# Three weight tiles in place of two, row by row, behind four of the six norms

## The reference

```python
hx = _modulate(_rms(x, norm_mix_g[i]), sx1, cx1)          # rms norm, then (1 + scale) * h + shift
x = x + gx1 * mixer(hx, ...)                              # layer 0: conv/Fourier; layer 1: attention
x = x + gx2 * _mlp(_modulate(_rms(x, norm_mlp_g[i]), sx2, cx2), mlp_w1[i], mlp_w2[i])
# _mlp(h, w1, w2) = square(relu(h @ w1)) @ w2
q = _rms(h @ w_q, g); k = _rms(h @ w_k, g)                # layer 1: norms per head
u = rms_norm(h, ab_pre_norm) @ ab_w_in                    # second model: gates, conv, rope, attention
# shift, scale and gate come from  cond @ ada_w[i] + ada_b[i]
```

## The kernel before

| norm | normc | norm | first projections | other groups |
|---|---|---|---|---|
| 1, before the MLP of layer 0 | 54 (pair 2) | 55 (pair 3) | up 0, 1, 2 = 56, 57, 58 (pairs 0, 1, 2) | up 3 = 59 |
| 2, before q and k of layer 1 | 168 (pair 0) | 169 (pair 1) | q 0, 1 = 170, 171 (pairs 2, 3), q 2 = 173 (pair 1) | qksum 0 = 172, qksum 1 = 174 |
| 3, before the MLP of layer 1 | 234 (pair 2) | 235 (pair 3) | up 0, 1, 2 = 236, 237, 238 (pairs 0, 1, 2) | up 3 = 239 |
| 4, before in3 | 332 (pair 0) | 333 (pair 1) | in3 0, 1, 2 = 334, 335, 336 (pairs 2, 3, 0) | in3 3 = 337 |

## Time and profile before

### The profile page before, as it was taken

The page is one execution under the profiler, slowest core; times in us unless marked ns, Lnnn a source line. Parts: engine busy times, 40 slices in busy tenths (PEclk is TensorE's granted clock), DMA queues, the critical chain, the costliest instruction groups (busy, mean ns, idle before and its releaser), DMA issues.

```text
span 2318.3 us, 33033 instructions
## 1 busy us (share of the span) xinstructions
PE 2149.3 (93%) x13426; PEld 1839.4 (79%) x13426; DVE 1218.6 (53%) x1594; ACT 786.0 (34%) x1267; POOL 675.3 (29%) x314
## 2 busy tenths in 40 slices
PE   5898989999999997999899999999999896999987
PEld 3687878888888885889777888888998695977766
DVE  3787658455565446560873322223788315066652
ACT  2212223122222124332873333222323533355542
POOL 0331313222222222222893444444021124200002
PEclk9998989999999999999999999999998897999998
DMA  7333324224332231221322333333221011211110
GB/s 282 125 128 117 121 72 138 99 84 151 100 127 90 94 100 45 72 60 46 56 45 80 103 95 93 94 96 91 73 83 55 10 55 45 75 55 56 55 46 36
DMA packets 74953, 199.92 MB, mean 86 GB/s; under 512 B 25296, under 2 KB 26576, under 8 KB 74832
## 3 DMA queue, kind: packets, MB, share of 16 engines
q1 hardware_dynamic: 73648, 197.60, 27.6%
q10 hardware_dynamic: 1184, 0.61, 0.1%
HBM read 194.51 MB, written 2.10 MB: 85 GB/s over the span
## 4 chain that ended last, share of the span: by engine, by line
PE 82%; DVE 8%; POOL 3%; issue 3%; ACT 2%; DMA 1%; SPq 0%; DVEq 0%; ACTq 0%
PE ps L2044 59%; PE ps L2159 5%; PE ps L2516 5%; PE ps L2059 3%; POOL NAP L856 2%; DVE ada_acc L1386 1%; PE ps L2069 1%; PE ps L2083 1%; PE ps L2220 1%; DMA ring<-stream 1%; PE ps L2540 1%; PE ps L2076 1%; DVE S L1454 1%; PE ps L2552 1%; DVE UC L1751 1%
## 5 line engine op out<-in xcount | busy, mean ns | idle before, releaser
L809 POOL TENSOR_TENSOR WL<-raw,WH 128x1024 fp32r<-128x1024 f32 x215 | 523.7, 2439 | 1349.7 <-ACT WH L906 1349.4
L906 ACT ACTIVATE WH<-raw 128x1024 fp32r<-128x1024 f32 x260 | 273.2, 1054 | 499.6 <-PE ps L2044 471.9
L2044 PE MATMUL ps<-HH,WH 128*128 128x512 f32 (+2 forms) x1568 | 423.8, 336 | 2.5 <-DVE HL L1853 2.5
L2044 PE MATMUL ps<-HH,WL 128*128 128x512 f32 (+2 forms) x1568 | 418.4, 333 | 0.0
L2044 PE MATMUL ps<-HL,WH 128*128 128x512 f32 (+2 forms) x1568 | 418.0, 333 | 0.0
L2044 PEld LDWEIGHTS ps<-HH,WH 128*128 128x128 f32 x1568 | 252.0, 188 | 37.6 <-issue 3.6
L2044 PEld LDWEIGHTS ps<-HL,WH 128*128 128x128 f32 x1568 | 251.6, 188 | 34.0 <-issue 1.4
L2044 PEld LDWEIGHTS ps<-HH,WL 128*128 128x128 f32 x1568 | 251.2, 188 | 31.2
L2044 PE MATMUL ps<-GH,WH 128*128 128x512 f32 (+1 forms) x896 | 266.0, 355 | 3.0 <-issue 3.0
L2044 PE MATMUL ps<-GH,WL 128*128 128x512 f32 (+1 forms) x896 | 266.6, 355 | 0.0
L2044 PE MATMUL ps<-GL,WH 128*128 128x512 f32 (+1 forms) x896 | 265.4, 354 | 0.0
(11 more groups left out here) (269 smaller groups left out, 3384.7 us busy)
## 6 DMA issues: line engine op xcount, KB each, us to landing
raw<-stream SPq DMA_DIRECT2D x260, 512.0 KB, 3.6
ring<-stream SPq DMA_DIRECT2D x80, 512.0 KB, 3.7
ADA<-stream SPq DMA_DIRECT2D x4, 2048.0 KB, 20.8
XT<-rpb SPq DMA_DIRECT2D x128, 24.0 KB, 2.4
XT<-xT SPq DMA_DIRECT2D x1, 2048.0 KB, 8.7
out<-XT SPq DMA_DIRECT2D x8, 256.0 KB, 2.0
V1s<-V SPq DMA_DIRECT2D x6, 256.0 KB, 4.6
XT<-ctxT SPq DMA_DIRECT2D x1, 1024.0 KB, 11.2
```

The source lines that it names most:

```text
L809: nc.gpsimd.tensor_tensor(WL[:, slot, :], raw[:, slot, :], WH[:, slot, :].bitcast(F32), ALU.subtract).then_inc(lo_done[slot], 1)
L906: nc.scalar.activation(WH[:, slot, :], raw[:, slot, :], ACT.Copy).then_inc(hi_done[slot], 1)
L2044: ins = nc.tensor.matmul(pair(g)[:, cols], lhs, x[:, k, cols], start=first, stop=last)
```

## The change

`project_two` is renamed `project_first` and is otherwise the same; it takes as many tiles as its list has. Behind norms 1 to 4 the list has three tiles in place of two, and the tile-by-tile projections begin one tile later. Behind norms 0 and 5 it has two as before. Only PE's program is changed: the list of groups, the loads and the programs of SP, ACT, DVE and POOL are as they were.

```diff
-            def project_two(items, h, r, between=lambda k, part: None):
+            def project_first(items, h, r, between=lambda k, part: None):
 
                 for g, tile, n in items:
                     weights(tile)
                     empty(g)
...
             def mlp_up(layer, c, q):
                 r = 1 + 2 * layer
                 for i in range(4):
-                    if c == 0 and i < 2:
+                    if c == 0 and i < 3:
                         if i == 0:
-                            project_two([(GROUP["up", layer, 0, j], TILE["up", layer, 0, j], MLP_N[layer]) for j in range(2)],
+                            project_first([(GROUP["up", layer, 0, j], TILE["up", layer, 0, j], MLP_N[layer]) for j in range(3)],
                                         MLP_H[layer], r)
...
             for i in range(16):
                 if i == 0:
-                    project_two([(GROUP["qk1", j], TILE["q1", j], NX) for j in range(2)], (HH2, HL2), 2)
-                elif i > 1:
+                    project_first([(GROUP["qk1", j], TILE["q1", j], NX) for j in range(3)], (HH2, HL2), 2)
+                elif i > 2:
                     project(GROUP["qk1", i], TILE["q1" if i < 8 else "k1", i % 8], (HH2, HL2), NX if i < 8 else N1)
                 if i:
                     qk_sum(i - 1)
...
             for i in range(22):
                 if i == 0:
-                    project_two([(GROUP["in3", j], TILE["in3", j], N2) for j in range(2)], H4, 4)
-                elif i > 1:
+                    project_first([(GROUP["in3", j], TILE["in3", j], N2) for j in range(3)], H4, 4)
+                elif i > 2:
                     project(GROUP["in3", i], TILE["in3", i], H4, N2)
```

More of the change, by code:

```diff
@@ L2180, in _ @@
                 if i == 0:
-                    project_two([(GROUP["in1", j], TILE["in1", j], N1) for j in range(2)], H1, 0, second_half)
+                    project_first([(GROUP["in1", j], TILE["in1", j], N1) for j in range(2)], H1, 0, second_half)
                 elif i > 1:
@@ L2495, in _ @@
             H5 = (HH5, HL5)
-            project_two([(GROUP["q4", 0], TILE["q4", 0], NX), (GROUP["k4", 0], TILE["k4", 0], N2)], H5, 5)
+            project_first([(GROUP["q4", 0], TILE["q4", 0], NX), (GROUP["k4", 0], TILE["k4", 0], N2)], H5, 5)
             for w in range(4):
```

## The result

The changed kernel takes 2340.43 us (median of 4 runs, 2337.92 to 2346.66), the kernel before, beside it, 2317.42 us (4 runs, 2316.68 to 2317.85). The ratio is 1.0104, with a 95% interval of 1.0086 to 1.0122: slower by 23.0 us by the medians and by 24.1 by the ratio (19.9 to 28.3 by its interval), where 18.4 were forecast. The sign is as forecast, and so are the two places of the loss. The size was put 5 to 6 us too small: the median lies just under the range's upper end of 2341, and the ratio applied to the earlier median (2341.8) just over it. The profiled execution took 2342.16 us, with a span of 2340.4 and a mean clock of 0.955.

What follows compares the result with a forecast made beforehand. PE, busy 93% of the span, was taken as the bound, so only its standing still counts. Losses of 13.7 + 4.7 + 0 + 0 = 18.4 us on the 2317.7 us median gave 2336.1 us, range 2330.5 to 2341.

Steps and rivals of the forecast that it cites:

- the two places of the loss: Behind norm 2, 13.7 us lost, and behind norm 1, 4.7 us lost; nothing behind norms 3 and 4.
- Norm 2: Behind norm 2 PE waits for DVE's release of `norm` before its first row, losing the overlap: 13.7 us slower.
- The climb: PE's return to full clock after standing still 23 us behind norm 2: 2.0 us, ends 1.6 to 2.7.
- Two readings ahead of these steps: L2059 waited 17.7 us for HH and HL over six norms; behind norm 2 each row's low part is awaited 1.03 us.
- Norm 1: Behind norm 1 up tiles end together, DVE starts products 8.0 us later and PE waits: 4.7 us, ends 2.0 and 8.0.
- the ring: Behind norm 1, DVE's loads wait for the product before last; with hand-over that stays, 1.2 us added.
- Norms 3 and 4: Behind these norms the cover is thick enough: cost 0, at most 1.9 and 2.3 us.
- Norm 2 alone: Rival: DVE catches up behind norm 1 or PE isn't held, only norm 2's 13.7 us remains: 2331.4 us; chance 0.12.
- All covers are thin: Rival: norm 1 costs 8.0, norm 3 1.9, norm 4 2.3, norm 2 14.9 us: 2344.8 us; chance 0.07.
- The free pair: Rival: third tile's PSUM pair is free at norm 2's start, winning 4.5 us there: 2317.9 or 2313.2 us; chance 0.05.

Runs made afterwards that it cites:

- The kernels with more matmuls: Kernel before plus 30 or 60 matmuls ahead of the third q tile behind norm 2, no wait added: ratios 1.0047 and 1.0079 to the kernel before.

## Why the prediction was wrong in its size, by its own steps

**Norm 2: right, 13.7 forecast, 13.8 and 14.2 measured** (in two pairs of profiles, each the change beside the kernel before). The whole kernel is 6.83 us later at norm 2's reciprocal (892.85 against 886.02), and with that taken off each point of the working can be laid beside the trace: PE starts at 911.91 (forecast 912.0), the last HL matmuls at 930.34 (930.1), tile 3 at 934.39 (934.3). The climb took 18.4 - 16.1 = 2.3 us where the mean of four windows gave 2.0. Nothing was regained behind it. Two readings ahead of these steps are loose, and enter no term: L2059 also waited 3.2 us for HH of L951, so its waits were 20.9 us over the six norms and not 17.7; and 1.03 us is the wait for the low part in five of the eight rows behind norm 2, not in each.

**Norm 1: this step failed, 4.7 forecast, 6.9 and 7.4 measured.** By 1.34 us the changed kernel is ahead at this norm's first row (329.32 against 330.66). With that added, DVE's first item is 7.94 us later (forecast 8.0), its products end at 415.42 against 410.33, 5.1 later (4.7), and L2130 starts 4.9 later. DVE caught up 2.9 us instead of 3.3, and the ring did become visible: DVE waited 0.67 and 0.78 us for its loads. Up to PE's start the step is right within 0.4 us. The term that was left out comes behind it: PE had stood still for 5.0 us and comes out of that wait at half clock. The windows from L2130's first matmul to the turn, of the kernel before and then of the change:

```profile
410.53:420.04 9.51, 9.51 (x65) 7.86 (x65) 3.71 (x8) 1.06 (x1) 2.40 (x1) 1.00 0.37 128
```
```profile
414.13:425.64 11.51, 11.51 (x64) 8.96 (x65) 3.86 (x8) 0.00 (x0) 2.17 (x1) 0.81 0.37 130
```

PE is busy for all of it in both, at clocks of 1.00 and 0.81, and the same matmuls take 2.0 us more. The prediction had this very figure, 2.0 us from the earlier trace rows, and charged it at norm 2, where a wait of 23 us stood in view. Behind norm 1 it put the climb at nothing, without a reason, though its own new wait there was 4.7 us long. 4.9 + 2.0 is 6.9 us. In the other three traces with that wait PE starts the sums 4.8 to 4.9 us late and the climb costs 2.6, 1.5 and 1.5 us. So the lateness was sized well four times, and the climb was missing each time.

**Norms 3 and 4: right**, 0 forecast, ratio 1.0001 measured.

**The rest stays open.** With a climb of 2.0 us behind norm 1 the sum would have been 20.4, and 24.1 us were measured. Of the two pairs of profiles (22.1 and 23.4 us longer) norm 1 takes 2.2 and 2.7 over its term and norm 2 0.1 and 0.5; 1.3 and 1.8 us are left over the sum of 18.4. They lie in no one stretch. In the first pair the start is 1.3 us shorter, the first MLP 1.2 and the stretch before norm 3 2.3 longer; in the second pair these are +2.0, -0.3 and 0.0. Two executions of one kernel differ in these stretches by up to 3.3, 1.2 and 1.6 us. The kernels with more matmuls show that a shift can cost extra without any wait (10.9 for 7.1, 18.3 for 14.0); whether and where the full change pays for its shift is not shown. The prediction had no term for it.

**The rivals.** "Norm 2 alone" fell: DVE caught up only 2.9 of 7.9 us, and PE was held. "All covers are thin" gave a time near the result (2344.8) for reasons that did not hold: norms 3 and 4 cost nothing and norm 1 did not reach 8.0. "The free pair" was not this kernel; built, it won 3.7 us behind norm 2 where 4.5 were said. The prediction cited the Trainium skill (TensorE: Matmul & The Clock Gate, Part 1) for the count of slow matmuls differing from run to run. This case agrees: one stretch of one kernel took 149.7 and 152.6 us at clocks of 0.88 and 0.87, and the climb behind norm 1 cost 1.5 to 2.6 us. But that there is a climb is no noise: it came in all four traces that have the wait (95.8, 95.8, 96.3 and 97.9 us for the stretch, against 89.4 and 90.6 in the two of the kernel before).

## What to carry to other kernels

- Before more tiles are taken together, list for each place the buffers that the larger group claims at its start and who frees each of them last. A claim made ahead of the loop turns one buffer into a wait for all of the work that the loop was to overlap with; here swapping the numbers of two groups turned +13.9 us into -3.7 behind norm 2.
- Wherever a forecast adds a wait of PE as long as these, add the clock's climb behind it too: here 1.5 to 2.6 us behind waits of 4.8 to 5.8 us, and 2.3 to 2.8 us behind waits of 22.5 to 22.7.
- What is produced together later also releases its consumers later: count how much the next engine has queued between that release and the point at which PE needs it.

## What the runs showed of the hardware

- A pause of PE more than four times as long costs hardly more climb: 1.5, 1.5, 2.0 and 2.6 us behind pauses of 4.8 to 5.8 us, 2.3 to 2.8 us behind four of 22.5 to 22.7 us (the time from the first matmul to the last, less that of the same matmuls at full clock).
- A stretch with many short gaps (1040 matmuls, some 17 to 19 us of PE idle in 150) takes 149.7 to 156.1 us, with clocks of 0.88 down to 0.83, though its instructions are the same; 149.7 and 152.6 are two executions of one kernel. The 6.4 us between the ends are more than the 0.2% (4.6 us) by which two kernels can be told apart. A change of a few us ahead of such a stretch is best read from its own stretch as well as from the whole time.
